# Causal mask of an attention's scores: added on VectorE, together with scaling and row maximum, instead of on TensorE

## The reference

```python
proj = rms_norm(h, attn_pre_g) @ w_in                 # queries, keys, values, latents
s = einsum('bhqd,bhkd->bhqk', q_blk, k) * scale       # scores
s = where(k_pos[None, :] <= q_pos[:, None], s, NEG_INF)
p = softmax(s, axis=-1)
o = einsum('bhqk,bhkd->bhqd', p, v)
h = h + rms_norm(mix @ w_out, attn_post_g)            # mix: the heads side by side
a = square(relu(rms_norm(h, mlp_pre_g) @ w_up))
h = h + rms_norm(a @ w_down, mlp_post_g)
```

## Time and profile before

| | |
|---|---|
| timed runs | 625.82, 627.37, 628.8 us |
| span of the profiled execution | 625.1 us (no other time of this execution is on record; the median of the runs is 2.3 us above its span) |
| PE busy | 613.4 us, 98% |
| PE weight loads busy | 505.6 us, 81% |
| DVE busy | 303.0 us, 48% |
| ACT busy | 268.5 us, 43% |
| POOL busy | 99.8 us, 16% |
| chain that ended last | PE 95% |
| score tiles computed | from 104.44 to 205.7 us |
| mask matmuls | 64, 230 ns each by their rows |

### The profile page before, as it was taken

How to read it: one execution, slowest core, us unless ns; L and a number is a source line. 1 busy time by engine, 2 the same in 40 slices (tenths; PEclk the granted TensorE clock), 3 DMA queues, 4 the chain that set the end, 5 groups by cost and what they waited for, 6 DMA issues and landing times.

```text
span 625.1 us, 8241 instructions
## 1 busy us (share of the span) xinstructions
PE 613.4 (98%) x3056; PEld 505.6 (81%) x3056; DVE 303.0 (48%) x555; ACT 268.5 (43%) x564; POOL 99.8 (16%) x167
## 2 busy tenths in 40 slices
PE   8999999999999999999999999999999999999996
PEld 7988888777777788898888888888888888888874
DVE  3457673788788506626353434434242332423344
ACT  5653342778787505454433434352321312213131
POOL 0253300445687300120000000000000000000011
PEclk9999999999999899999999999999999999999999
DMA  8432321000110076002424232233223132231203
GB/s 301 136 110 84 135 77 59 1 2 0 68 69 2 1 239 191 8 2 68 134 67 134 67 122 80 87 114 116 86 76 126 67 131 70 71 130 67 101 16 120
DMA packets 32826, 55.24 MB, mean 88 GB/s; under 512 B 3232, under 2 KB 21408, under 8 KB 32800
## 3 DMA queue, kind: packets, MB, share of 16 engines
q1 hardware_dynamic: 31760, 54.90, 26.2%
q10 hardware_dynamic: 1040, 0.00, 0.1%
HBM read 52.80 MB, written 2.10 MB: 88 GB/s over the span
## 4 chain that ended last, share of the span: by engine, by line
PE 95%; DVE 1%; DMA 1%; ACT 1%; issue 1%; SPq 0%; DVEq 0%; POOLq 0%; POOL 0%; ACTq 0%
PE bank L915 31%; PE bank L917 29%; PE bank L916 29%; PE bank L1086 3%; PE bank L1053 1%; DMA x_sb<-in_x 1%; PE bank L1022 1%; PE bank L921 1%; PE bank L954 1%; DVE pT_lo L637 1%; DVE mx L766 0%; PE bank L1038 0%; ACT probs L503 0%; PE bank L980 0%; DVE kT_lo L637 0%
## 5 line engine op out<-in xcount | busy, mean ns | idle before, releaser
L915 PE MATMUL bank<-uT_hi,w_hi 128*128 128x512 f32 (+1 forms) x280 | 104.0, 371 | 0.0
L916 PE MATMUL bank<-uT_lo,w_hi 128*128 128x512 f32 (+1 forms) x280 | 103.8, 371 | 0.0
L917 PE MATMUL bank<-uT_hi,w_lo 128*128 128x512 f32 (+1 forms) x280 | 103.8, 371 | 0.0
L915 PE MATMUL bank<-w_hi,a_hi 128*128 128x512 f32 x256 | 101.2, 395 | 0.0
L916 PE MATMUL bank<-w_lo,a_hi 128*128 128x512 f32 x256 | 101.1, 395 | 0.0
L917 PE MATMUL bank<-w_hi,a_lo 128*128 128x512 f32 x256 | 101.1, 395 | 0.0
L637 DVE TENSOR_TENSOR w_lo<-w_raw,w_hi 128x2048 fp32r<-128x2048 f32 (+1 forms) x17 | 38.4, 2261 | 116.3 <-ACT w_hi L391 116.3
L391 ACT ACTIVATE w_hi<-w_raw 128x2048 fp32r<-128x2048 f32 (+2 forms) x25 | 37.0, 1490 | 123.1 <-PE bank L917 122.3
L640 DVE SCALAR_TENSOR_TENSOR w_lo<-w_raw,g_up,w_hi 128x256 fp32r<-128x256 f32 x128 | 52.1, 480 | 47.4 <-ACT w_hi L391 47.4
L915 PE MATMUL bank<-w_hi,uT_hi 128*128 128x512 f32 (+1 forms) x160 | 62.0, 387 | 0.0
L601 ACT ACTIVATE relu<-bank 128x512 f32<-128x512 f32 x32 | 19.1, 597 | 98.2 <-PE bank L917 98.2
(11 more groups left out here) (129 smaller groups left out, 950.2 us busy)
## 6 DMA issues: line engine op xcount, KB each, us to landing
w_raw<-in_w_up SPq DMA_DIRECT2D x16, 1024.0 KB, 5.5
w_raw<-in_w_down SPq DMA_DIRECT2D x16, 1024.0 KB, 4.9
w_raw<-in_w_in SPq DMA_DIRECT2D x6, 1024.0 KB, 5.4
w_raw<-in_w_out SPq DMA_DIRECT2D x4, 1024.0 KB, 4.9
x_sb<-in_x SPq DMA_DIRECT2D x8, 256.0 KB, 5.9
h_sb<-in_x SPq DMA_DIRECT2D x4, 512.0 KB, 5.4
out<-h_sb SPq DMA_DIRECT2D x8, 256.0 KB, 2.0
w_raw<-in_w_in SPq DMA_DIRECT2D x2, 416.0 KB, 5.1
```

Of the source, the lines that this page charges most:

```text
L915: nc.tensor.matmul(out, lh, rh, start=start, stop=False)
L916: nc.tensor.matmul(out, lh, rl, start=False, stop=False)
L917: return nc.tensor.matmul(out, ll, rh, start=False, stop=stop)
```

## The change

The mask becomes a float32 tile of 128 x 512: zero, with the causal triangle (-1e30) in its last 128 columns. A tile of width w reads the last w columns of it. The bf16 matmul goes, and `mm3` now ends the accumulation. On DVE one operation reads the whole score tile and the mask, adds them, multiplies by -scale, writes the result back over the tile in PSUM, and takes the minimum of it, which is the former `nb`. So `mx`, the wait of DVE for its own maxima, and the `nb` operations go. ACT's scale becomes -1. There are four signals `s_nb` per head instead of two: ACT can start tile 1 once tile 1 is done; for tiles 0 and 2, which share a bank, it waits for all four. DVE gets a wait for the exponential of two heads before, because `nb` is written by each tile apart. The scratch for DMA descriptors that POOL would write is made smaller, to make room for the mask; no DMA is issued by POOL.

```diff
-        mask_b = sb("mask_b", [P, P], BF16)
+        mask = sb("mask", [P, TOP])
...
-            nc.gpsimd.memset(mask_b[:, :], 0.0).then_inc(zeroed, 1)
+            nc.gpsimd.memset(mask[:, :], 0.0).then_inc(zeroed, 1)
...
-            nc.gpsimd.affine_select(out=mask_b[:, :], in_=mask_b[:, :], compare_op=ALU.is_ge, fill=NEG, base=0,
+            nc.gpsimd.affine_select(out=mask[:, TOP - P:], in_=mask[:, TOP - P:], compare_op=ALU.is_ge, fill=NEG, base=0,
                                     pattern=[[-1, P]], channel_multiplier=1).then_inc(consts, 1)
...
-                    act.wait_ge(s_nb, 2 * i + (1 if j == 0 else 2))
+                    act.wait_ge(s_nb, NT * i + (j + 1 if j < 2 else NT))
...
-                                         bias=nb[:, i % 2, t:t + 1], scale=SCALE[i],
+                                         bias=nb[:, i % 2, t:t + 1], scale=-1.0,
...
-                    last = nc.vector.reduce_max(mx[:, i % 2, t:t + 1], ps[b][:, c:c + P * (t + 1)], AX_X)
-                    if n in (0, 3):
-                        step(last)
-                        w = slice(t, t + 1) if n == 0 else slice(0, 3)
-                        nc.vector.tensor_scalar(nb[:, i % 2, w], mx[:, i % 2, w], -SCALE[i], None,
-                                                ALU.mult).then_inc(s_nb, 1)
+                    if i >= 2:
+                        dve.wait_ge(s_exp, NT * (i - 2) + n + 1)
+                    s = ps[b][:, c:c + P * (t + 1)]
+                    nc.vector.tensor_tensor_reduce(out=s, in0=s, in1=mask[:, TOP - P * (t + 1):], scale=-SCALE[i],
+                                                   scalar=-NEG, op0=ALU.add, op1=ALU.min,
+                                                   accum_out=nb[:, i % 2, t:t + 1]).then_inc(s_nb, 1)
...
-                    mm3(ps[b][:, c:c + w], qT_hi[s][r, tok], qT_lo[s][r, tok], kT_hi[s][r, 0:w], kT_lo[s][r, 0:w],
-                        True, False)
-                    last = nc.tensor.matmul(ps[b][:, c + w - P:c + w], ident_b[:, :], mask_b[:, :], start=False, stop=True)
+                    last = mm3(ps[b][:, c:c + w], qT_hi[s][r, tok], qT_lo[s][r, tok], kT_hi[s][r, 0:w], kT_lo[s][r, 0:w],
+                               True, True)
...
-    nc = bacc.Bacc("TRN2", target_bir_lowering=False, num_devices=1)
+    nc = bacc.Bacc("TRN2", target_bir_lowering=False, num_devices=1, dynamic_dma_scratch_size=1024)
```

More of the change, by code:

```diff
@@ L22 @@
 ACT = mybir.ActivationFunctionType
-AX_X = mybir.AxisListType.X
 P = 128
@@ L115, in build @@
         kT_lo = [sb(f"kT_lo{i}", [P, S], F32R, stack=att) for i in range(2)]
-        mx = sb("mx", [P, 2, NT], stack=att)
         nb = sb("nb", [P, 2, NT], stack=att)
```

## The result

The changed kernel takes 616.55 us (median of four runs, 616.42 to 616.86), the kernel before 626.60 us on the same chip. The ratio is 0.983, with a 95% interval of 0.981 to 0.985. The forecast was 618.4, and 9.0 us less than before; measured are 10.05 less.

The account below looks back on a forecast made before the run. The prediction took PE as the bound: 11.4 us freed there, 9.0 of it passing, so span 625.1 - 9.0 = 616.1, and 2.3 from span to median gives 618.4 us. Its own range was 615.5 to 621.5, the full range 614 to 626.

Parts of the forecast that it names:

- What bounds the kernel: PE sets the pace, busy 613.4 of 625.1 us; the other engines follow at 78 to 87% of it.
- What PE loses: Gaps around the mask matmuls: 1.02 us a MoBA head and 0.41 an MLA head go, 11.4 us in all.
- The dearer exit: Behind a MoBA head's last tile: the row switch moves onto the next matmul, so only 0.90 us a head goes.
- What DVE gets: Per head, four new operations at 1.8 us and write-outs at 0.3, about 2.1 us; DVE's load unchanged.
- My lower bound: On DVE, if the write-out is hidden in the next operation, DVE gains 0.15 to 0.3 us.
- How much passes: 0.8 of 1.02 us passes per MoBA head, 0.3 of 0.41 in MLA heads 2-7, all in 0-1: 9.0 us.
- rival B: Gain stays in the queues: MLA turns keep 6.42 us, MoBA turns fall to about 6.0; 623 us, chance 0.17.
- Edits at nothing: The `s_exp` wait, longer memset (a few tenths at most before PE's first matmul) and scratch size count as nothing.
- The sum: Whole kernel: profiled span 625.1 less 9.0 gives 616.1 us; with 2.3 from span to median, 618.4 us.

Follow-up runs that it names:

- e3: Kernel before, with the MoBA heads' mask matmul on the 64 rows the head uses instead of 128 (half of the mask left out): 625.03 us.
- e1: Kernel before without the mask matmul (causal mask left out), DVE's maxima and bias operations as before: 623.06 us.
- e10: Kernel before without the mask matmul (causal mask left out), the bias operation also summing its row into a spare column: 618.65 us.
- e5: Changed kernel with one more DVE maximum over 512 mask columns per head, about 0.6 us, result unused: 619.99 us.
- e7: Changed kernel with ACT's exponentials of tiles 3 and 1 earlier in MoBA turns and the mask's memset behind the identities: 615.54 us.
- e2: Changed kernel with the bf16 mask matmul kept, so the mask is added twice: 626.07 us.
- e4: Changed kernel with ACT waiting for all four minima before tile 1's exponential, as before the change: 617.09 us.
- e8: Changed kernel with a tensor_scalar over 3 SBUF columns per head ahead of tile 2's operation, result unused: 618.37 us.
- e9: Changed kernel with a maximum over 3 columns per head ahead of tile 2's operation, result unused: 616.83 us.

## Why the prediction was right, and where it was not

**What bounds the kernel.** Right. PE set the pace, and the others were close behind: in the MoBA window ACT is now at 89%, POOL at 86% and DVE at 83%. For DVE the prediction had 97%.

**What PE loses.** Right, per gap and per kind. All the gaps became those of their like, and e3 shows that the switch of rows makes three fifths of a MoBA mask's price. The dearer exit did not come: in head 8's turn, with PE busy throughout, 1.03 us went (6.58 to 5.55), where the sum had 1.02.

**What DVE gets.** The term was mis-sized. I had equality for the operation (it takes 695 instead of 672 ns for 512 columns, and 330 instead of 282 for 128) and 0.08 us of slot for each write-out. The write-outs take no slot, so the stretch from tile 3 to the key became 1.75 us, where I had 2.1. My lower bound had 0.15 to 0.3 us less; that is what was measured. With the stalls gone as well, DVE's busy time in the MoBA window fell from 37.16 us to 33.27, 0.56 a turn, where I had it unchanged.

**How much passes.** 0.75 of 1.02 us a MoBA turn (forecast 0.8), 0.28 of 0.41 an MLA turn of heads 4 to 6 (forecast 0.3). The numbers are near, but the reason was wrong in one step: I counted nothing for the stalls of the bias operation and took the gain for PE's time alone. e1 shows that without DVE's part nothing passes in the MLA turns of heads 4 to 6 and 0.53 of 1.02 us in a MoBA turn. Two covers had to go as well: the stall on POOL, harmless only while PE came late (e10: 4.4 us, of which 2.9 are not the clock), and the chain from maximum to key (2.1 us from e10 to the changed kernel), which e5 shows to be the bound of an MLA turn nearly one for one. At equal clock 4.2 (e1), 2.9 (e10) and 2.1 us add up to about the 9.3. What I gave as rival B, the gain kept back in the queues, is what e1 is; DVE's half of the change is what prevents it.

**Edits at nothing.** The longer memset was not free: 0.20 us up to the first score matmul, which e7 takes back.

**How near the number is.** The sum started from a profiled span, 625.1 us, that holds one stretch at half clock (about 1.4 us), and added 2.3 us from span to time; in the changed kernel's four runs time less span is 1.9 to 2.0. These two make most of the 1.85 us between forecast and result, and neither is of the mechanism. The rest nearly cancels, which is in part luck: heads 0 to 7 gave 3.1 us where the sum had 2.6, the MoBA heads 5.9 (5.29, and 0.6 of the 2.03 in head 15's) where it had 6.4, and the start took 0.2.

**The clock.** The half-speed stretch of the earlier trace rows did not occur in the changed kernel's profile. About 1.4 of the 10.2 us between the profiles are this, and 0.8 of the 10.05 between the medians, as the steps below show. In e2 such a stretch fell in one turn. Windows of the turn before it and of its own; the last number but two is the granted clock:

```profile
175.72:182.29 6.57, 6.57 (x43) 4.93 (x42) 4.97 (x15) 5.19 (x15) 4.31 (x6) 1.00 0.48 161
182.29:190.37 8.08, 8.08 (x43) 5.94 (x43) 4.98 (x16) 5.67 (x19) 6.15 (x7) 0.79 0.00 0
```

With the same 43 matmuls the turn took 1.5 us more. The 23 runs of the kernel before beside e1 to e4 fall into steps of about that size: three at 625.9 us with a mean clock of 0.998 or more, ten at 627.0 to 627.5 with 0.995 or 0.996, ten at 628.7 to 630.7 with 0.992 or 0.993. The changed kernel's four runs all had 0.997 or more. At equal clock the gain is 625.9 less 616.6, 9.3 us. Why the changed kernel has no such stretch stays open: all six runs of e1, without any mask matmul, had a mean clock of 0.996 or less, and its profile has one; e10, which differs from e1 only in the bias operation, has four runs at 0.997 or more and no such stretch in its profile's attention stage. Nor do the traces show one state of PE ahead of it: PE was busy throughout before the clock fell in the kernel before and in e2, and for 3.65 of the 4.40 us before it fell in e1 (173.00 to 177.40).

## What to carry to other kernels

Price a small matmul by the starts around it, not by its columns: one of 128 columns cost up to 0.35 us in a MoBA head, three fifths of it because it changed the rows in use; behind it the next weights were loaded late. When the bound engine is relieved, look for stalls on its neighbours that cost nothing so far; they are paid from then on, and an edit that shortens both sides can be worth much more than the sum of its halves (here 9.3 us against 5.3). Measure each half alone before you credit one. And read the granted clock of every window before you compare two: in e1 one stretch of 3.4 us hid two fifths of what the MoBA turns had gained.

## What was not expected of the hardware

- A DVE `tensor_scalar` over three columns of SBUF waits until a running POOL operation ends (1.28 us for 0.16 of work; e8 shows by the end times that it waits). The same operation with an accumulator output (e10, 153 to 156 ns) and a maximum over three columns (e9, 147 to 158 ns) do not. The Trainium skill, SBUF — State Buffer, section Who interferes with whom, says that `tensor_scalar` can take the port pair shared with GpSimd, as an exclusive lock, and excepts the form that writes out its accumulator; the trace agrees, with 1.28 us and 153 to 156 ns.
- The read of DVE's accumulator shows 140 ns and delays the next operation by nothing, while behind ACT's, at 201 ns, the next operation starts about 0.09 us later (in the kernel before, read at 169.51 us, next copy at 169.60).
- A fused operation that reads PSUM and SBUF and writes back into the same PSUM columns costs 695 ns for 512 columns, 11 ns more than the one of the earlier trace rows that writes to SBUF (684).
- A 128-row matmul between 64-row ones costs PE 0.09 us in front of it (0.32 instead of 0.23) and 0.12 behind it (0.16 instead of 0.04), at 2.4 GHz; with the same bf16 type on 64 rows both are gone (e3).
- A stretch of 3.4 us at half clock costs 1.5 us in a turn of 6.57 (e2). By the steps of time and mean clock it comes in some executions of the kernel before and not in others.
